# Sample attention: a stick chunk's weights are turned in the third tick behind its scores instead of the second

## The chip, the cores and the metric

The kernel runs on one core of a Trainium2 chip. The metric is device time in microseconds (us), median of several runs. The engines are named as in the profile: PE is TensorE (PEld its weight loads), DVE is VectorE, ACT is ScalarE, POOL is GpSimd, SP is SyncE, which only issues DMAs here. Each engine works through its own list of instructions in the order in which the program was written; between engines only semaphores hold.

## The reference, cut to what matters

Two decoder layers run over 512 prompt tokens and 64 sample tokens (8 requests of 8). Each layer is a SwiGLU FFN, a token mixing with four head groups (mLSTM, GLA, dilated window attention, stick-breaking attention), and a second FFN. The change touches only the sample's attention, whose stick-breaking part is this, for keys of 2048 past positions in pages and 8 new ones:

```python
z = q @ k.T * HEAD_DIM ** -0.5 + bias
log_beta = where(valid, log_sigmoid(z), -inf)
log_keep = where(valid, log_sigmoid(-z), 0)
later = cumsum(log_keep, reverse=True) - log_keep
out = exp(log_beta + later) @ v
```

## The kernel before

`program` loops twice (`nc.Fori`) over `ffn`, `mixing`, `ffn`. `mixing` projects, and then runs four stages one after the other, each closed by a barrier of all engines: `mlstm`, `rotary`, `gla` and `prompt_attention`. Those are the main work. Beside them the sample's attention is woven in as **side work**, cut into 62 ticks: `weave` writes, on each engine, some steps of the main stage, then the side ticks that `paced` assigns to that place, then main steps again. Ticks 0 to 25 lie in `mlstm`, 26 and 27 in `rotary`, 28 to 39 in `gla`, 40 to 61 in `prompt_attention` (`PACE`). So the order on an engine is fixed in the source, and a side instruction that waits holds up the main instruction behind it.

The side work takes four passes: stick-breaking for requests 0 to 3 and 4 to 7, then window attention for the same two groups. A **unit** is one tile of 128 past positions; tick t turns the keys of unit t. Four units of a stick pass form a **chunk** (m), scored into one PSUM bank; the new positions are a chunk of their own. In the order of a tick:

- PE: `turn_keys` (L2382, eight transposes, half into bank a, half into bank b), `score_unit` for the unit before (L2399), `turn_weights` of a chunk if its turn is due (L2429), `gather_rows` one tick behind the end of a pass (L2461), and `value_unit` (L2448, or L2442 for new positions).
- ACT: copy of bank a's keys (L2493), Exp of the chunk whose scores came the tick before (L2512), then Abs, Exp, Ln of a chunk just scored (L2518, L2520, L2522), the copy of the turned weights for an even m (L2501), the copy of the gathered rows (L2532).
- DVE: copy of bank b's keys (L2552), the running sum of the chunk before (L2598, L2601, L2604), the reading of a chunk's scores (L2579, L2570), the copy of the turned weights for an odd m (L2560), the output rows of a pass that ends (L2632).
- SP: the values of unit n + 4 are loaded when unit n has been multiplied (L2319, L2307). POOL gathers the keys of unit t + 4.

Bank a and bank b are one PSUM bank each. Keys and turned weights share them, so `turn_weights` waits until the keys of its own tick have been copied out of its bank, and the keys of the next tick wait until the weights have been copied out. `copy_weights_a` and `copy_weights_b` are these copies.

When a chunk is turned is decided in `side_plan`. A stick chunk m has its tick (1, 4, 8, 12, 16 in the first pass; 17, 20, 24, 28, 32 in the second), in which its scores are read. Its weights are `a_ready` when ACT has done L2512, one tick on. The plan is `turn_at` (before: ticks 3, 6, 10, 14, 18 and 19, 23, 26, 30, 34), and `value_at` has the products of a chunk in the four ticks behind its turn. The main lines that matter: L1497, L1518 (mLSTM, PE), L1462 (its Exp, ACT), L1399 (its product, DVE), L1210 and L1197 (the turning of a stage's result at its end, PE and ACT), L1129/L1131 (rotary, PE), L1821 (GLA, PE), L1735 and L1844 (GLA, DVE and PE), L1995, L2037 and L2057 (prompt attention).

Of the kernel before, what the change touches and what calls it, by code (L numbers as in the profile page):

```python
# [2152 lines left out]
def side_plan():  # L2153

    passes, units, chunks = [], [], []
    nth = {"stick": 0, "window": 0}
    for p, (kind, g) in enumerate(SIDE_ORDER):
        window = kind == "window"
        tiles = WIN_TILES if window else N_PAGES
        groups = [tuple(range(c, min(c + UT, tiles))) for c in range(0, tiles, UT)]  # L2160
        groups = groups + [()] if window else [()] + groups[::-1]
        first, unit0 = len(chunks), len(units)
        end = unit0 + tiles
        for k, group in enumerate(groups):
            m = len(chunks)
            tick = len(units) + len(group)
            if not group and not window:
                tick += 1
            chunks.append(dict(m=m, p=p, k=k, new=not group, window=window, g=g, tiles=group, unit0=len(units),
                               tick=tick, stick=None if window else nth["stick"], first=k == 0,  # L2170
                               last=k == len(groups) - 1, width=len(group) * P if group else NS))
            if not window:
                nth["stick"] += 1
            units += [(m, i, t) for i, t in enumerate(group)]
        passes.append(dict(kind=kind, window=window, g=g, unit0=unit0, end=end, chunk0=first, chunks=len(groups),
                           row=nth["window"] if window else None))
        if window:
            nth["window"] += 1


    turn_at, value_at, unit_at = {}, {}, [None] * len(units)
    done = []
    t_value = t_turn = 0
    for c in chunks:
        q = passes[c["p"]]
        ready = chunks[q["chunk0"] + q["chunks"] - 1]["tick"] + 2 if c["window"] else c["tick"] + 2
        t = max(ready, t_turn, done[c["m"] - 2] if c["m"] >= 2 else 0)
        turn_at.setdefault(t, []).append(c["m"])
        t_turn = t
        t_value = max(t_value, t + 1)  # L2190
        if c["new"]:
            value_at.setdefault(t_value, []).append((c["m"], None))
        for i in range(len(c["tiles"])):
            n = c["unit0"] + i
            value_at.setdefault(t_value, []).append((c["m"], n))
            unit_at[n] = t_value
            if t_value < len(units) or i % 2 == 1:
                t_value += 1
        done.append(t_value)
    ends = {}  # L2200
    for t in sorted(value_at):
        for m, n in value_at[t]:
            if chunks[m]["last"] and (n is None or n == chunks[m]["unit0"] + len(chunks[m]["tiles"]) - 1):
                ends[t] = chunks[m]["p"]
    ticks = max(ends) + 2


    events = {"a": {}, "b": {}}
    for t in range(ticks):
        if t < len(units):  # L2210
            for bank in "ab":
                events[bank]["k", t] = len(events[bank])
        for m in turn_at.get(t, ()):
            bank = "ab"[m % 2]
            events[bank]["p", m] = len(events[bank])
        if t - 1 in ends:
            events["a"]["g", ends[t - 1]] = len(events["a"])
    scored = {}
    for t in range(1, len(units) + 1):
        q = passes[chunks[units[t - 1][0]]["p"]]  # L2220
        if not q["window"] and t - 1 == q["unit0"]:
            scored["new", q["chunk0"]] = len(scored) + 1
        scored["unit", t - 1] = len(scored) + 1
        if q["window"] and t == q["end"]:
            scored["new", q["chunk0"] + q["chunks"] - 1] = len(scored) + 1
    valued = {}
    for t in sorted(value_at):
        for m, n in value_at[t]:
            valued["new", m] = valued["unit", n] = len({v for v in valued.values()}) + 1
    return dict(passes=passes, units=units, chunks=chunks, turn_at=turn_at, value_at=value_at, ends=ends, ticks=ticks,  # L2230
                events=events, scored=scored, valued=valued)


def sample_attention(nc, st, E, M, l, I, C):

    ps = E["ps"]
    DQT, DKT = M["TR"][:, DQ:DQ + 2, :], M["TR"][:, DK:DK + H, :]
    G = side_plan()
    passes, units, chunks = G["passes"], G["units"], G["chunks"]
    U, NP_ = len(units), len(G["passes"])  # L2240
# [723 lines left out]
```

## Time and profile before

| what | us |
|---|---|
| median of 3 runs | 2821.46 |
| lowest, highest | 2819.78, 2826.64 |
| the profiled execution's own time | 2828.29 |
| its span from first to last instruction | 2826.7 |
| PE busy | 2430.4 (86%) |
| DVE busy, ACT busy | 1249.8 (44%), 923.7 (33%) |

The profile is one execution. Its page gives sums for each engine and a row of digits in 40 slices of 70.7 us; the mixings with the side work lie in slices 9 to 14 and 28 to 34. All else comes from the timeline, which lists instructions by start, duration, engine and line, and says for some what the engine waited for. Start times in the text are those of the first layer.

### The profile page before, as it was taken

What the parts mean: (1) busy time and instruction counts of PE and PEld (TensorE: products, weight loads), DVE (VectorE), ACT (ScalarE), POOL (GpSimd) and SP (SyncE); (2) the same over time, 40 slices, a digit from 0 to 9 for tenths busy, and PEclk for the clock granted to TensorE, in tenths of its full rate; (3) what the DMA queues carried; (4) which work ended last, traced back from release to release, by engine and by line L of the source; (5) the groups of instructions that cost most, each with busy time, mean ns of one, the idle gap of its engine ahead of it and who ended that gap; (6) DMA issues with size and microseconds to landing.
All of it is one profiled execution on the core that took longest, in us unless ns stands there. A gap on an engine that the chain in (4) does not pass through costs nothing. (4 is left out here: it accounts for less than half of the span.)

```text
span 2826.7 us, 45166 instructions
## 1 busy us (share of the span) xinstructions
PE 2430.4 (86%) x17622; PEld 2140.8 (76%) x17622; DVE 1249.8 (44%) x2054; ACT 923.7 (33%) x1617; POOL 208.5 (7%) x279
## 2 busy tenths in 40 slices
PE   5999979969687877999879998898885786889996
PEld 5999968746445576999879998876563464889996
DVE  6433273143565536333354334521555555463324
ACT  4222232123424544222242223221343254432222
POOL 2000020011122001000010000100111110000000
PEclk7999989979787998999979999999896788899998
DMA  3223213155544442233223231322564444322332
GB/s 95 78 76 97 77 44 112 45 159 161 149 143 140 127 124 57 74 78 90 61 61 81 76 95 54 102 75 76 161 184 127 143 119 117 104 60 74 89 90 64
DMA packets 364348, 278.34 MB, mean 98 GB/s; under 512 B 51680, under 2 KB 347784, under 8 KB 363664
## 3 DMA queue, kind: packets, MB, share of 16 engines
q1 hardware_dynamic: 348048, 221.52, 27.8%
q0 software_dynamic: 16128, 54.54, 6.5%
q8 instruction: 106, 1.74, 0.3%
q14 instruction: 66, 0.54, 0.1%
HBM read 262.41 MB, written 13.58 MB: 98 GB/s over the span
## 5 line engine op out<-in xcount | busy, mean ns | idle before, releaser
L216 PE MATMUL ps<-h_hi,w_hi 128*128 128x288 f32 x2400 | 739.5, 308 | 133.6 <-PEq L172 47.2
L217 PE MATMUL ps<-h_lo,w_hi 128*128 128x288 f32 x2400 | 724.6, 302 | 0.0
L218 PE MATMUL ps<-h_hi,w_lo 128*128 128x288 f32 x2400 | 723.8, 302 | 0.0
L216 PEld LDWEIGHTS ps<-h_hi,w_hi 128*128 128x128 f32 x2400 | 465.6, 194 | 152.7 <-issue 71.7
L217 PEld LDWEIGHTS ps<-h_lo,w_hi 128*128 128x128 f32 x2400 | 466.9, 195 | 1.2
L218 PEld LDWEIGHTS ps<-h_hi,w_lo 128*128 128x128 f32 x2400 | 466.2, 194 | 0.0
L240 DVE TENSOR_TENSOR w_lo<-w_raw,w_hi 128x2048 fp32r<-128x2048 f32 x133 | 306.5, 2305 | 299.1 <-ACT w_hi L234 299.0
L234 ACT ACTIVATE w_hi<-w_raw 128x2048 fp32r<-128x2048 f32 x133 | 253.4, 1905 | 167.8 <-PE ps L218 161.3
L216 PE MATMUL ps<-f_a_hi,w_hi 128*128 128x288 f32 x1024 | 302.7, 296 | 0.0
L218 PE MATMUL ps<-f_a_hi,w_lo 128*128 128x288 f32 x1024 | 301.6, 295 | 0.0
L217 PE MATMUL ps<-f_a_lo,w_hi 128*128 128x288 f32 x1024 | 301.5, 294 | 0.0
L696 ACT ACTIVATE f_gate<-f_gate 128x288 f32<-128x288 f32 x128 | 56.9, 444 | 473.7 <-DVE f_gate L726 473.6
L216 PEld LDWEIGHTS ps<-f_a_hi,w_hi 128*128 128x128 f32 x1024 | 192.0, 188 | 0.4
L217 PEld LDWEIGHTS ps<-f_a_lo,w_hi 128*128 128x128 f32 x1024 | 192.0, 188 | 0.2
L218 PEld LDWEIGHTS ps<-f_a_hi,w_lo 128*128 128x128 f32 x1024 | 192.0, 188 | 0.0
L2382 PE MATMUL ps<-ident,sa_kn 128*128 128x128 f32 x832 | 140.3, 322 | 38.2 <-DMA sa_kn<-in_cache_sb_k,page_rows 14.9
L726 DVE TENSOR_TENSOR f_gate<-ps,f_inv_x 128x288 f32<-128x288 f32 x128 | 58.5, 457 | 233.5 <-PE ps L218 233.3
L2382 PEld LDWEIGHTS ps<-ident,sa_kn 128*128 128x128 f32 x832 | 115.2, 169 | 60.9 <-issue 36.8
L394 POOL TENSOR_TENSOR A<-A,f_x_sq 128x288 f32<-128x288 f32 x56 | 44.7, 798 | 1323.2 <-ACT f_x_sq L384 1323.2
L216 PE MATMUL ps<-w_hi,h_hi 128*128 128x512 f32 (+1 forms) x320 | 126.7, 396 | 0.0
L2552 DVE COPY sa_kt<-ps 128x512 f32<-128x512 f32 x104 | 71.7, 690 | 124.1 <-PE ps L2382 121.6
L217 PE MATMUL ps<-w_lo,h_hi 128*128 128x512 f32 (+1 forms) x320 | 124.9, 390 | 0.0
(348 smaller groups left out, 3357.9 us busy)
## 6 DMA issues: line engine op xcount, KB each, us to landing
w_raw<-in_w_ffn_in SPq DMA_DIRECT2D x132, 512.0 KB, 5.2
w_raw<-in_w_ffn_out SPq DMA_DIRECT2D x64, 512.0 KB, 4.9
sa_vn<-in_cache_sb_v SPq DMA_DIRECT2D x256, 128.0 KB
w_raw<-in_w_in SPq DMA_DIRECT2D x52, 512.0 KB, 4.6
sa_kn<-in_cache_win_k POOLq DMA_DIRECT2D x96, 128.0 KB, 3.3
sa_vn<-in_cache_win_v SPq DMA_DIRECT2D x96, 128.0 KB
sa_kn<-in_cache_win_k POOLq DMA_DIRECT2D x16, 512.0 KB, 4.8
sa_vn<-in_cache_win_v SPq DMA_DIRECT2D x16, 512.0 KB
```

Source lines behind the costliest of these rows:

```text
L216: pe.matmul(out, stat_hi, mov_hi, start=start, stop=False, skip_group_check=True)
L217: pe.matmul(out, stat_hi, mov_lo, start=False, stop=False, skip_group_check=True)
L218: return pe.matmul(out, stat_lo, mov_hi, start=False, stop=stop, skip_group_check=True)
L234: act.activation(E["w_hi"][:, slot], E["w_raw"][:, slot], ACT.Copy).then_inc(S["w_hi"], 1)
L240: dve.tensor_tensor(E["w_lo"][:, slot], E["w_raw"][:, slot], E["w_hi"][:, slot].bitcast(F32), ALU.subtract).then_inc(S["w_lo"], 1)
L394: pool.tensor_tensor(E["acc_x"][:, hs], E["acc_x"][:, hs], F["xsq"][:, N.adds(n) % 2], ALU.add).then_inc(S["x_added"], 1)
L696: act.activation(gate[:, j, :], gate[:, j, :], ACT.Silu).then_inc(S["silu_done"], 1)
L726: dve.tensor_tensor(gate[:, j, :], E["ps"][:, PAIR[j], 0:HALF], inv_x[:, half_of(j // 2)], ALU.mult).then_inc(S["scaled"], 1)
L2382: mm = pe.transpose(ps[:, banks[e % len(banks)], j * P:(j + 1) * P], kn[:, n % SLOTS, j, pair * P:(pair + 1) * P], E["ident"][:])
L2552: dve.tensor_copy(kt[:, n % 2, 1], ps[:, TURN_B[e % len(TURN_B)], :]).then_inc(S["free_b"], 1)
```

## The change

One number of the plan: a stick chunk is ready to be turned three ticks after its scores, not two. The new positions' chunks are stick chunks too. Window chunks keep their rule.

```diff
@@ side_plan
     for c in chunks:
         q = passes[c["p"]]
-        ready = chunks[q["chunk0"] + q["chunks"] - 1]["tick"] + 2 if c["window"] else c["tick"] + 2
+        ready = chunks[q["chunk0"] + q["chunks"] - 1]["tick"] + 2 if c["window"] else c["tick"] + 3
         t = max(ready, t_turn, done[c["m"] - 2] if c["m"] >= 2 else 0)
         turn_at.setdefault(t, []).append(c["m"])
```

The ten stick turns then stand in ticks 4, 7, 11, 15, 19, 20, 24, 27, 31 and 35, all stick products one tick later than before, the ends of the two stick passes in ticks 23 and 40 instead of 22 and 39, and their gathers in 24 and 41 instead of 23 and 40. From tick 44 on everything stands where it stood, and there are 62 ticks as before. Nothing is added or removed. Keys, scores, Exp, Ln and sums keep their ticks; POOL's list is the same.

**PE at the end of `mlstm`, ticks 23 to 25, before** (L1578 and L1210 are main, the rest side):

```order
L2382 MATMUL ps<-ident,sa_kn 128x128 x8
L2399 MATMUL ps<-sa_kt,sa_qb 32x128 x8
L2429 MATMUL ps<-ident,sa_zs 128x128 x4
L2461 MATMUL ps<-sa_gather,sa_rows 128x32 x2
L2442 MATMUL ps<-RB,sa_pT 128x256
L1578 MATMUL ps<-ident,A 4x64
L1579 MATMUL ps<-ident,sa_zw 16x128
L2382 MATMUL ps<-ident,sa_kn 128x128 x8
L2399 MATMUL ps<-sa_kt,sa_qb 32x128 x8
L2448 MATMUL ps<-sa_vn,sa_pT 32x256 x4
L1210 MATMUL ps<-ident,ml_room 128x128 x8
```

The same stretch of the change:

```order
L2382 MATMUL ps<-ident,sa_kn 128x128 x8
L2399 MATMUL ps<-sa_kt,sa_qb 32x128 x8
L2448 MATMUL ps<-sa_vn,sa_pT 32x256 x4
L1578 MATMUL ps<-ident,A 4x64
L1579 MATMUL ps<-ident,sa_zw 16x128
L2382 MATMUL ps<-ident,sa_kn 128x128 x8
L2399 MATMUL ps<-sa_kt,sa_qb 32x128 x8
L2429 MATMUL ps<-ident,sa_zs 128x128 x4
L2461 MATMUL ps<-sa_gather,sa_rows 128x32 x2
L2442 MATMUL ps<-RB,sa_pT 128x256
L1210 MATMUL ps<-ident,ml_room 128x128 x8
```

The turn of chunk 6, the gather of the first pass and the product of chunk 5 moved from the tick ahead of L1578 to the tick ahead of L1210.

**ACT at the same place**, as a piece of the difference:

```order
 L2522 ACT_TABLE_LOAD
 L2522 ACTIVATE sa_f<-sa_f 128x512
+L2501 ACTIVATE sa_pT<-ps 128x512
+L2532 ACTIVATE TR<-ps 128x2x32
 L1197 ACTIVATE TR<-ps 128x128 x8
 L1197 ACTIVATE TR<-ps 128x64 x2
```

The two copies that belong to them now stand behind the Ln of chunk 7 (L2522) and ahead of the main copies L1197.

**PE at the start of `gla`'s main products, ticks 30 and 31** (L1821 is main):

```order
 L2382 MATMUL ps<-ident,sa_kn 128x128 x8
 L2399 MATMUL ps<-sa_kt,sa_qb 32x128 x8
+L2448 MATMUL ps<-sa_vn,sa_pT 32x256 x4
+L2382 MATMUL ps<-ident,sa_kn 128x128 x8
+L2399 MATMUL ps<-sa_kt,sa_qb 32x128 x8
 L2429 MATMUL ps<-ident,sa_zs 128x128 x4
-L2448 MATMUL ps<-sa_vn,sa_pT 32x256 x4
-L2382 MATMUL ps<-ident,sa_kn 128x128 x8
-L2399 MATMUL ps<-sa_kt,sa_qb 32x128 x8
 L2448 MATMUL ps<-sa_vn,sa_pT 32x256 x4
 L1821 MATMUL ps<-ident,A 128x128
```

The turn of chunk 8 moved behind the keys and scores of the next tick; both ticks stand ahead of L1821 either way.

## Rows read from the trace of the kernel before

**Rows 1.** The page: PE's granted clock in 40 slices, in tenths of 2.4 GHz.

```profile
PEclk7999989979787998999979999999896788899998
```

**Rows 2.** Windows, ticks 0 to 51 of each layer: length, busy by engine, clock, DMA.

```profile
584.08:945.40 361.32, 278.31 (x2371) 189.02 (x2370) 193.84 (x419) 138.57 (x298) 58.64 (x84) 0.82 0.52 153
1969.93:2336.63 366.70, 278.69 (x2371) 187.64 (x2370) 194.05 (x419) 138.48 (x298) 58.51 (x84) 0.82 0.52 151
```

**Rows 3.** Line L2429: what ended PE's idle time before it (us, times).

```profile
  issue: 45.9, 24
  ACT sa_kt L2493: 21.3, 6
  DVE sa_kt L2552: 14.4, 6
```

**Rows 4.** Timeline, ticks 3 and 4: start, duration, engine, line [idle <-releaser].

```profile
607.29 0.39 PE L2429 MATMUL ps<-ident,sa_zs 128*64 128x128 f32 x1 [4.77 <-ACT sa_kt L2493]
...
608.13 1.94 PE L2382 MATMUL ps<-ident,sa_kn 128*128 128x128 f32 x8 [0.45 <-ACT sa_pT L2501]
...
611.13 1.22 PE L2442 MATMUL ps<-RB,sa_pT 64*128 64x256 f32 x2
...
612.28 0.87 PEld L1497 LDWEIGHTS ps<-ident,ml_room 4*128 4x128 f32 x8 [0.65 <-issue]
```

**Rows 5.** Timeline, ticks 6 and 7.

```profile
625.68 0.63 PE L2429 MATMUL ps<-ident,sa_zs 128*128 128x128 f32 x4 [1.91 <-DVE sa_kt L2552]
...
626.35 0.69 DVE L2560 COPY sa_pT<-ps 128x512 f32<-128x512 f32 x1 [0.81 <-PE ps L2429]
...
630.11 0.61 PE L1518 MATMUL ps<-ml_mask,ident 128*128 128x128 f32 x2
...
631.07 0.68 DVE L2552 COPY sa_kt<-ps 128x512 f32<-128x512 f32 x1
```

**Rows 6.** Timeline, tick 24 and the end of `mlstm`.

```profile
738.62 0.69 PE L1210 MATMUL ps<-ident,ml_room 128*128 128x128 f32 x2 [6.36 <-DVE ml_room L1181]
739.11 0.63 ACT L2522 ACTIVATE sa_f<-sa_f 128x512 f32<-128x512 f32 x1
739.65 0.42 ACT L1197 ACTIVATE TR<-ps 128x128 f32<-128x128 f32 x2
739.96 0.69 PE L1210 MATMUL ps<-ident,ml_room 128*128 128x128 f32 x2 [0.65 <-ACT TR L1197]
740.47 0.49 ACT L1197 ACTIVATE TR<-ps 128x128 f32<-128x128 f32 x2 [0.40 <-PE ps L1210]
```

**Rows 7.** Timeline, tick 26, in `rotary`.

```profile
757.75 1.02 DVE L1095 TENSOR_TENSOR x<-ro_tmp 128x256 f32<-128x256 f32 x4
...
759.53 0.63 PE L2429 MATMUL ps<-ident,sa_zs 128*128 128x128 f32 x4 [4.03 <-DVE sa_kt L2552]
...
761.10 0.48 PE L1129 MATMUL ps<-ident,x 128*128 128x128 f32 x1
```

**Rows 8.** Timeline, ticks 30 and 31, in `gla`.

```profile
789.30 0.64 ACT L2512 ACTIVATE sa_zs<-sa_zs 128x512 f32<-128x512 f32 x1 [3.35 <-DVE sa_zs L2604]
...
794.83 1.09 PE L2429 MATMUL ps<-ident,sa_zs 128*128 128x128 f32 x4 [5.08 <-ACT sa_kt L2493]
...
796.87 1.97 PE L2382 MATMUL ps<-ident,sa_kn 128*128 128x128 f32 x8
...
800.74 0.46 PE L1821 MATMUL ps<-ident,A 128*128 128x128 f32 x1
```

**Rows 9.** Timeline, ticks 34 and 35, in `gla`.

```profile
828.75 1.45 PE L1837 MATMUL ps<-x,gl_room 64*128 64x256 f32 x4 [0.41 <-DVE gl_room L1735]
...
834.08 0.27 DVE L1735 COPY gl_room<-ps 64x128 f32<-64x128 f32 x1
```

**Rows 10.** Timeline, end of pass 1 in tick 39, and its gather in tick 40.

```profile
863.84 0.41 DVE L2632 TENSOR_TENSOR sa_rows<-ps,sa_head_cols 128x256 f32<-128x256 f32 x1
...
878.16 1.06 PE L2461 MATMUL ps<-sa_gather,sa_rows 128*128 128x32 f32 x4
```

## The prediction

> **What bounds the kernel now.** I read the page's clock row first, then windows over the two mixings, then the answer for line L2429, then the timeline around each of the ten stick turns, in both layers. The clock row shows where engines wait for each other: it is 9 in the FFNs and falls to 7 and 8 in the mixings, since PE's clock falls to 1.2 GHz where PE has idled [rows 1]. Over ticks 0 to 51 PE is busy for 278 of 361 us, DVE for 194, ACT for 139 [rows 2]. No engine is full there: PE's own list sets the pace in the middle of `mlstm`, and a chain through DVE and ACT does so at the start and the end of each stage. What a moved turn is worth therefore depends on which engine is late at its old and its new place.
>
> The change gives the weights' Exp a tick more. I looked whether that is what the turn waits for. It is not. For chunk 8, Exp ends at 789.94 and the turn starts at 794.83 [rows 8]; in all 20 stick turns of both layers, Exp ends 2.7 to 10.5 us ahead. What the turn waits for, where it waits, is the copy that empties its bank of the keys of its own tick: ACT's L2493 or DVE's L2552 [rows 3]. Both come late only where those engines have main work ahead of them. In the first layer this is 4.77 us in tick 3 [rows 4], 1.91 in tick 6 [rows 5], 4.03 in tick 26 [rows 7] and 5.08 in tick 30 [rows 8]; at the other six turns PE stands still for at most 0.4 us. A turn in the next tick waits for the copy of that tick's keys by the same rule. So the change replaces waits, it doesn't remove a dependency.
>
> **The change, place by place.** Times are of the first layer; each sum is a shift of the main work behind it, plus is later.
>
> Ticks 3 to 7, the start of `mlstm`. With no turn in tick 3 the keys of tick 4 still wait for the same bank; they start where the turn started, 607.29, not at 608.13: -0.85 [rows 4]. From tick 4 the product of chunk 0 goes (L2442 to the next start, 1.15) and the turn comes in (about 0.35), so L1497 starts 1.65 sooner; the product stands in tick 5 now and takes 1.15 back. That leaves -0.5. In tick 6 DVE is the late engine: it loses the copy L2560 and the wait ahead of it (0.69 + 0.81 = 1.5), so its key copy of tick 7, which ends at 631.75, ends at 629.75 [rows 5]. There the turn now waits for it: 629.75 + 0.15 + 0.65 = 630.55 for L1518, which starts at 630.11 now. **+0.4.** The 0.15 is the step from a copy to PE, 0.65 the turn's own length [rows 5].
>
> Ticks 10 to 20, PE sets the pace. Each of the turns of chunks 2 to 5 leaves a tick where it costs PE its own 0.65 and enters one where it costs the same; the copies find ACT and DVE with room in both. Zero. If that room were gone at one of them, it is one copy, 0.6 to 0.7, as in tick 6 [rows 5].
>
> Tick 24, the end of `mlstm`. This is the largest term. Turn 6, the gather and the product of chunk 5 were in tick 23, where PE had time to spare while DVE normalised. Now they stand between the scores of tick 24 and L1210. Turn 6 itself fits: L1210 waits for DVE until 738.62 in any case. But its copy L2501 is written behind the Abs, Exp and Ln of chunk 7 on ACT, with two table loads among them, and Ln ends at 739.74 [rows 6]. The gather needs the same bank and must wait for L2501. Before, ACT went from Ln straight to L1197. Now follow: L2501 about 0.6, the step to PE 0.15, the gather 1.06 at the low clock [rows 10], the product of chunk 5 1.15 [rows 4], and 0.5 from the start of L1210 to ACT's L1197 (739.96 to 740.47 [rows 6]). The sum, 0.6 + 0.15 + 1.0 + 1.15 + 0.5, is **+3.4**: L1197 starts at 743.1 instead of 739.65. Everything to the stage's end hangs on it: keys 25, their product, SP's last value load, the barrier. At its cheapest (the gather and product at 2.4 GHz, half as long) it is 2.3; nothing hides it, since the two L1210 that were done early are now behind it.
>
> Ticks 26 and 27, `rotary`. L1129 needs only DVE's L1095, which ends at 758.77, but stands behind the turn, which waits until 759.53, and the product, and starts at 761.10 [rows 7]. Without the turn the product is done in the idle time, and L1129 starts at 758.95: -2.15. In tick 27 the turn finds its bank copied and costs its 0.65. **-1.5.**
>
> Ticks 30 and 31, `gla`. PE stands for 5.08 us until ACT has copied key tile 30, then works off turn, product, keys 31 (1.97), scores, product, and reaches L1821 at 800.74 [rows 8]. The change does the product in the idle time, but keys 31 wait for the same copy. They start at 794.85 instead of 796.87, and the turn (1.09) and one product (1.0) follow them: 794.85 + 1.95 + 1.1 + 1.1 + 1.0 = 800.0 for L1821. Of 5.08 us of idle time the change wins **-0.7**.
>
> Ticks 34 and 35, `gla`. Tick 34 loses the wait, the turn and with them 1.35 us ahead of L1837 (828.75, could start at 827.4 [rows 9]). Tick 35 gets them: 0.15 + 0.65 on PE, then DVE copies the weights (0.69) ahead of L1735, so that this starts at 835.6 instead of 834.08 [rows 9]; +1.55. **+0.2.**
>
> Ticks 40 and 41, `prompt_attention`. The pass's last product takes the gather's place on PE, about as long as its 1.06 [rows 10], but DVE's L2632 (0.41) must wait for it ahead of the main L2037: 0.4 of wait and 0.4 of work. The gather comes into tick 41 ahead of L1995, 1.06, of which DVE is late by more than half anyway: 0.45. **+1.25.** The nearest bounds are 0 (this stage hides both) and 1.9.
>
> The sum is 0.4 + 3.4 - 1.5 - 0.7 + 0.2 + 1.25 = +3.05 per layer, **+6.1 us** for both layers, since all waits stand in the second layer too. On the profiled execution (2828.29) that gives 2834.4, and on the median of the runs, 6.8 below it, 2821.46 + 6.1 = **2827.5 us**.
>
> What this can't contain is where PE's clock falls. The same 2371 matmuls of ticks 0 to 51 took 361.32 us in one layer and 366.70 in the other, at the same mean clock [rows 2]. So the places at which the low clock lands are worth about 5 us per mixing, in either direction, and any shift of a few us moves them.
>
> **The rivals.** A measurement of this kernel tells about 0.3% from no change, 8.5 us, so the bounds are 2813.0 and 2829.9.
>
> *Slower: the losses count and the gains don't.* The mechanism is the one of tick 24: a copy of turned weights that stands behind chunk 7's table functions on ACT and holds L1210. It decides if the -2.15 of tick 26 and the -0.7 of tick 31 are absorbed, for instance if `rotary` ends on SP's value load rather than on PE. Then a layer pays 0.4 + 3.4 + 0.65 + 0.2 + 1.25 = 5.9, both 11.8: 2833. From 4.2 per layer on it is a loss that can be measured; the sum stands at 3.05, so 1.2 us more per layer is enough, and the clock's share alone is larger. For it speaks that all its terms are lists in strict order; against it that PE and DVE, not SP, work last in `rotary`.
>
> *Faster: the idle time was the bound.* The four waits and the two small ones of a layer sum to 16.2 us; at the new places I find 2.4 (tick 7) and 3.6 (tick 24), 6.3 in all. If the main work followed PE's idle time one for one, 9.9 per layer would be won: 2801.7. Against it: keys 4 and keys 31 wait for the same copies that the turns waited for [rows 4, 8]. A part of it, 4.2 per layer, would be enough to be seen.
>
> The row that bears on the clock is this: at 794.83 a turn takes 1.09 after 5.08 idle, the same turn in tick 6, after 1.91 idle, takes 0.63 [rows 5, 8]. The Trainium skill (TensorE: Matmul & The Clock Gate, "What's actually happening") says that the throttled state is the default and that activity releases it; by that rule a plan with less idle time on PE in ticks 3, 26 and 30 would win beyond the waits. As a mechanism here: if the keys of ticks 4, 25 to 28 and 31 ran at the high clock (1.09 for 1.97, 0.9 each) and the products with them, some 5 to 8 us per layer; with the sum above that is 2818 to 2812. Against it stands tick 24, where PE idles longer than before, until 740.5.
>
> *The change does nothing of note* is inside the forecast: a layer's sum near zero gives 2821.5.
>
> **How the numbers follow.** The forecast, within 0.3%, has 0.53: its sum of +6 leaves 2.4 us to the upper bound and 14.5 to the lower, with 5 to 7 us of scatter by the clock. Slower has 0.35, nearly all of it from the tick 24 mechanism with the clock against it. Faster has 0.12: 0.04 for the idle time as the bound, 0.08 for the clock's gain. The range, 8 in 10, reaches from the sum less 12.5 (the gains in full, tick 24 at 2.3, the last stage hiding its part, a layer's clock in favour) to the sum plus 11.5 (the slower rival with a layer's clock against): 2815 to 2839.
>
> **What would show it.** In tick 24, L2501 should start as Ln ends, L2461 0.75 later, and L1210 some 4 us later against the stage's start than before; if L2501 comes before Ln, the largest term is wrong. L1129 in tick 26 should follow L1095 at once. PE's idle time ahead of L2429 should fall from 21.3 and 14.4 us to a few, with L2382 named in its stead for ticks 4 and 31. If L1497 to L1518 shift by more than 1 us, the first term is wrong. The prediction as a whole fails if the two mixings change by over 4 us each.

## The result, and the profile after

The changed kernel takes 2836.64 us (median of 13 runs, 2828.33 to 2850.22). The kernel before takes 2824.84 us beside it (13 runs, 2816.38 to 2828.03). The ratio is 1.0046, with a 95% interval of 1.0033 to 1.0060: slower by about 12 us, a loss that can be told from no change. A second timing, in another batch, gave 1.0038 (1.0022 to 1.0054). The forecast was 2827.5 us. The time lies in its range, but it is the rival "slower" that came about, not the likeliest case.

The profiled execution of after took 2829.22 us (span 2827.6), 7 us under its median; the one of before took 2828.29. So this pair of traces shows the places, but not the full size of the loss. The change was traced a second time, in an execution of 2838.02 us, close to its median; where that trace says something else, it is named. First the page's clock row of after, then its windows over ticks 0 to 51 in each layer (columns as in [rows 2]: length, PE, PEld, DVE, ACT and POOL busy, granted clock, DMA share, GB/s).

```profile
PEclk7999989969786988999979999999797897899998
```

```profile
582.15:952.45 370.30, 284.44 (x2371) 193.94 (x2370) 194.27 (x419) 138.30 (x298) 58.78 (x84) 0.80 0.51 149
1974.14:2336.19 362.05, 271.08 (x2371) 185.06 (x2370) 193.93 (x419) 138.16 (x299) 58.81 (x84) 0.84 0.53 153
```

The same 2371 matmuls: 370.30 us against 361.32 in the first layer, 362.05 against 366.70 in the second [rows 2]. One layer lost 9.0 us and the other won 4.65. PE's busy time goes the same way (284.44 and 271.08, before 278.31 and 278.69), and so does the clock, 0.80 and 0.84 of full speed. Two layers of one execution differ by 8.25 us, about as much as the change moved either of them. In the second trace the same two stretches took 367.15 and 367.85 us: 5.8 and 1.2 us more than before, 7.0 in all.

Next, what ended PE's idle time before the turns (L2429), and before the key transposes (L2382), in after:

```profile
  ACT sa_kt L2493: 9.9, 6
  DVE sa_kt L2552: 6.2, 4
```

```profile
  ACT sa_kt L2493: 26.4, 10
  DVE sa_kt L2552: 12.7, 11
```

and the second of these in before:

```profile
  DVE sa_kt L2552: 8.6, 8
  ACT sa_kt L2493: 6.1, 6
```

Before the turns the wait for the two copies fell from 35.7 us [rows 3] to 16.1, of which 8.8 stand at chunk 6's new place in tick 24, 4.40 in each layer. Before the keys it rose from 14.7 to 39.1. In all 50.4 us became 55.2: the wait wasn't removed, it went over to the next instruction that needs the bank. (Idle time without a releaser went the same way, 45.9 to 26.0 us before the turns and 36.8 to 55.4 before the keys.)

**The start.** Keys 4, the first main line, and the main line of tick 7 (start, duration, engine, line, idle time and releaser):

```profile
605.52 1.94 PE L2382 MATMUL ps<-ident,sa_kn 128*128 128x128 f32 x8 [4.74 <-ACT sa_kt L2493]
...
608.88 1.12 PE L1497 MATMUL ps<-ident,ml_room 4*128 4x4 f32 x10
```

```profile
628.63 0.64 PE L1518 MATMUL ps<-ml_mask,ident 128*128 128x128 f32 x2
629.06 1.91 PE L1520 MATMUL ps<-ml_arow,ml_sel 128*128 128x512 f32 x2
```

The first layer's list starts 1.93 us sooner than in before (keys 0 at 581.00 and 582.93). On before's scale L1497 stands at 610.81 (worked out: 610.63) and L1518 at 630.56 (worked out: 630.55). In this layer these steps held to 0.2 us. In the second layer L1497 comes 1.8 us sooner than in before, and L1518 1.8 us later, where the sum had 0.4; before's own two layers have L1518 at 47.18 and 46.09 us from their keys 0. So that the first layer fits to 0.01 us is luck in part. Over all traces the term holds in the mean: 46.65 us in the fourteen layers with the first pass late, 46.19 in the twelve with before's first pass, +0.46 (the kernels are those of the experiments below; the one that alters tick 7 isn't counted).

What the sum didn't have is the line behind it. L1520 takes 1.91 us in tick 7 here; this is the same line in before:

```profile
630.55 1.02 PE L1520 MATMUL ps<-ml_arow,ml_sel 128*128 128x512 f32 x2
```

The clock was still low when the main work came. In thirteen of those fourteen layers this L1520 took 1.88 to 1.92 us, in one 1.02 (second trace, second layer); in the twelve others 1.02 to 1.40.

**Tick 24.** ACT's table functions, the copy behind them, the gather, the product of chunk 5, L1210 and L1197:

```profile
742.53 0.63 ACT L2522 ACTIVATE sa_f<-sa_f 128x512 f32<-128x512 f32 x1
743.07 0.58 ACT L2501 ACTIVATE sa_pT<-ps 128x512 f32<-128x512 f32 x1
...
743.79 1.03 PE L2461 MATMUL ps<-sa_gather,sa_rows 128*128 128x32 f32 x4 [4.20 <-ACT sa_pT L2501]
744.75 1.22 PE L2442 MATMUL ps<-RB,sa_pT 64*128 64x256 f32 x2
...
745.90 0.69 PE L1210 MATMUL ps<-ident,ml_room 128*128 128x128 f32 x2
746.41 0.49 ACT L1197 ACTIVATE TR<-ps 128x128 f32<-128x128 f32 x2 [1.33 <-PE ps L1210]
```

From the end of Ln (743.16) to L1197 are 3.25 us; the sum had 3.4.

**Rotary and `gla`.** L1129 now follows L1095 (which ends at 765.43) at once; from the start of `rotary` it stands at 6.6 us, 2.3 sooner than in before, where the sum had 2.15. In tick 31, keys, turn, product and L1821:

```profile
765.48 0.33 PE L1129 MATMUL ps<-ident,x 128*128 128x128 f32 x1 [2.48 <-DVE x L1095]
```

```profile
799.86 1.94 PE L2382 MATMUL ps<-ident,sa_kn 128*128 128x128 f32 x8 [5.87 <-ACT sa_kt L2493]
...
802.86 1.11 PE L2429 MATMUL ps<-ident,sa_zs 128*128 128x128 f32 x4
803.91 1.08 PE L2448 MATMUL ps<-sa_vn,sa_pT 128*32 128x256 f32 x8
804.92 0.34 PE L1821 MATMUL ps<-ident,A 128*128 128x128 f32 x1
```

As foreseen the keys have taken over the turn's wait (5.87, before 5.08 ahead of the turn [rows 8]). Against the stage's start L1821 comes 0.5 us sooner.

**What the lists don't say.** The same stage a little later, tick 33: first the first layer of after, then the second.

```profile
822.07 2.49 PE L1837 MATMUL ps<-x,gl_room 64*128 64x256 f32 x4 [2.68 <-DVE gl_room L1735]
...
824.49 1.97 PE L1844 MATMUL ps<-x,gl_room 128*128 128x64 f32 x8
```

```profile
2212.30 1.45 PE L1837 MATMUL ps<-x,gl_room 64*128 64x256 f32 x4 [2.67 <-DVE gl_room L1735]
2213.68 1.10 PE L1844 MATMUL ps<-x,gl_room 128*128 128x64 f32 x8
```

Same instructions, same idle time ahead, one execution; 4.46 us in one layer, 2.55 in the other. The one ran at the low level of the clock (1.2 GHz), the other at the high one (2.4 GHz). What did differ is the stretch ahead: in the first layer turn 8 and its product took 1.11 and 1.08 us, and L1821 started 28.4 us after the stage's start, in the second 27.3. This goes together in all fourteen traces of this document: where L1821 stood at 27.1 to 27.5 us, this L1837 took 1.45 (fourteen layers); where it stood at 27.9 to 29.2, it took 2.4 to 2.5 (thirteen layers, and one exception with 1.45). It is a regularity; no run here changed one of the two alone. `gla` as a whole took 96.34 and 92.47 us, in before 96.98 and 98.00.

**Ticks 41 and 42, `prompt_attention`.** After, and then the two lines of before that answer to its second and fourth:

```profile
891.91 1.06 PE L2461 MATMUL ps<-sa_gather,sa_rows 128*128 128x32 f32 x4
892.79 0.77 PE L1995 MATMUL ps<-TR 128*128 128x128 f32 x2
893.36 0.95 PE L2014 MATMUL ps<-RB,pa_pT 128*128 128x64 f32 x4
...
897.72 1.92 PE L2382 MATMUL ps<-ident,sa_kn 128*128 128x128 f32 x8
```

```profile
887.07 0.49 PE L1995 MATMUL ps<-TR 128*128 128x128 f32 x2
...
890.77 1.05 PE L2382 MATMUL ps<-ident,sa_kn 128*128 128x128 f32 x8
```

From this L1995 to keys 42 there are 4.93 us in after and 3.70 in before. The gather itself (1.06, ahead of this L1995) is one loss; that the lines behind it run at the low clock (L1995 0.77 for 0.49, and so on to keys 1.92 for 1.05) is a second, of the same size. In the second layer of this trace the lines behind the gather ran at the high clock, and from keys 41 to keys 42 only 0.4 us were lost, against 2.6 in the first; both layers of the second trace lost 2.4 to 2.6.

### The profile page after: what moved, and what is told of

Its sections match the earlier page's. It is cut to its first block and busy times, and to the rows that moved or that the text cites. A ratio compares the mean times of both kernels' runs of the same rounds, so it can differ in the third digit from the quotient of the medians.

```text
span 2827.6 us, 45166 instructions
## 1 busy us (share of the span) xinstructions
PE 2426.6 (86%) x17622; PEld 2140.7 (76%) x17622; DVE 1250.3 (44%) x2054; ACT 923.5 (33%) x1617; POOL 209.2 (7%) x279
## 3 DMA queue, kind: packets, MB, share of 16 engines
q1 hardware_dynamic: 348048, 221.52, 27.9%
## 5 line engine op out<-in xcount | busy, mean ns | idle before, releaser
L2382 PE MATMUL ps<-ident,sa_kn 128*128 128x128 f32 x832 | 141.4, 324 | 61.4 <-ACT sa_kt L2493 26.4
L2382 PEld LDWEIGHTS ps<-ident,sa_kn 128*128 128x128 f32 x832 | 116.6, 170 | 83.5 <-issue 55.4
```

Of the source, the lines that this page charges most:

```text
L2382: mm = pe.transpose(ps[:, banks[e % len(banks)], j * P:(j + 1) * P], kn[:, n % SLOTS, j, pair * P:(pair + 1) * P], E["ident"][:])
```

## The experiments

Each kernel ran in five rounds beside the kernel before, on the same chip as it; there were four batches, on three chips. A difference between kernels of two batches is therefore taken from their two ratios. The edits are in `side_plan`, where not said otherwise. "Gives 5 us" is the ratio times 2825.

**Parts of the change.** The start alone: the first pass's chunks 0 to 5 are turned a tick later, and the last two products of chunk 4 share tick 22, so that nothing moves from tick 23 on.

```diff
-        ready = ... c["tick"] + 2
+        ready = ... c["tick"] + (3 if c["m"] < 6 else 2)
-            if t_value < len(units) or i % 2 == 1:
+            if n != 14 and (t_value < len(units) or i % 2 == 1):
```

> Only the first pass's chunks 0 to 5 are turned a tick later (ticks 4, 7, 11, 15, 19, 20); two products share tick 22, so that the pass still ends in tick 22, turn 6 and the gather stay in tick 23, and everything behind stands as in the kernel before. It is the first term alone. Theory of the lists (a turn costs what waits in its list): L1518 in tick 7 comes 0.4 us later and the rest of mlstm keeps that, at most 1.1 with the second product in tick 22: +1 to +2 us in all, a ratio of 1.0005. Theory of the clock (the idle time moved to tick 7 puts mLSTM's first products at 1.2 GHz): from tick 7 to tick 12 another 3 to 4 us per layer, as in the profile of the change (keys of tick 12 are 4.3 and 4.2 us late there), +8 to +9 us in all, a ratio of 1.003.

Measured: 1.0018 (1.0007 to 1.0029), +5 us, between 2 and 8. Where the sum had +0.8 for both layers, and the shared tick 22 could add little, the start costs several times that. Its one trace, of its fastest execution (2823.65 us), doesn't show the loss: its two mixings are as long as before's.

The second pass alone, `(3 if c["m"] >= 6 else 2)`. Chunk 6 stays in tick 23, since its turn waits for the products of chunk 4 in any case; so chunks 7, 8 and 9 move, and no product does.

> Only the second pass's chunks 6 to 9 are ready a tick later. Chunk 6 stays in tick 23, since it waited for chunk 4's products already; chunks 7, 8 and 9 are turned in ticks 27, 31 and 35; no product moves. These are the terms of rotary and gla alone: -1.5 (ticks 26, 27), -0.7 (30, 31), +0.2 (34, 35), so -2.0 per layer, -4 us in all, a ratio of 0.9986. In the profile of the change rotary was 1.98 and 1.91 us shorter and gla 0.64 and 5.5; if that holds, -5 to -8 us. If the gain was only the barrier's (rotary short since mlstm ended late), rotary stays at 19.6 us and the ratio at 1.

Measured: 0.9964 (0.9952 to 0.9977), -10 us. This part of the change is a gain, two and a half times the sum's -4.0. Tick 31 in its first layer:

```profile
793.28 1.94 PE L2382 MATMUL ps<-ident,sa_kn 128*128 128x128 f32 x8 [4.53 <-ACT sa_kt L2493]
...
796.29 0.67 PE L2429 MATMUL ps<-ident,sa_zs 128*128 128x128 f32 x4
796.88 0.64 PE L2448 MATMUL ps<-sa_vn,sa_pT 128*32 128x256 f32 x8
797.45 0.33 PE L1821 MATMUL ps<-ident,A 128*128 128x128 f32 x1
```

The list is after's; turn and product take 0.67 and 0.64 for 1.11 and 1.08. The clock rose before them here, and behind them there. `gla` took 93.51 and 92.64 us.

The change with ACT's copy of the turned weights written ahead of Abs, Exp and Ln:

```diff
+        for m in G["turn_at"].get(t, ()):
+            if m % 2 == 0:
+                copy_weights_a(act, chunks[m])
         ... Abs, Exp, Ln of weighed_at(t, 0) ...
-        for m in G["turn_at"].get(t, ()):
-            if m % 2 == 0:
-                copy_weights_a(act, chunks[m])
```

> The change, with ACT's copy of turned weights (L2501) written ahead of Abs, Exp and Ln of its tick instead of behind them. In tick 24 the copy then follows the turn at about 736.4, the gather is released 4 us sooner, and L1210 may start by 738.7; what is left is that Ln, and so L1197, comes 1.1 us later. Theory of the lists: the 3.4 us of tick 24 fall to 1.1 per layer, 4.6 us less than the change in all, a ratio of about 1.003 to the kernel before; mlstm ends 2.3 us sooner than in the change. Rival (L1210 is held by the gather and the product of chunk 5 themselves, not by the place of the copy): mlstm's end as late as in the change.

Measured: 0.9999 (0.9985 to 1.0013). Writing the copy first gives back 11 to 13 us of the change's loss, where the list had 4.6. The queue behind Ln is a real cost, but not all of this: from keys 23 to keys 25 the trace has 20.96 us, the change 22.74 and before 19.38. That is 1.8 us a layer won in tick 24 (the list: 2.3), 3.6 in all. The rest lies in other stretches and isn't explained by the list.

The change with the keys of unit 7 transposed twice over (no work left out):

```diff
-            for j in range(SG):
+            for j in tuple(range(SG)) * (2 if n in (7,) else 1):
```

> The change, with the eight key transposes of tick 7 done twice (same data, same bank), so that PE works in the 2.4 us in which it waits for DVE there. Nothing else is added, and the second set ends before DVE's key copy can (DVE is late at that place), so the lists cost nothing, or 0.5 us at most. Theory of the clock: PE keeps or regains 2.4 GHz at L1518, the keys of tick 12 are 2 to 4 us less late than in the change, and the time falls by up to 8 us, to a ratio of 1.001 to 1.003. Theory of the lists, or of a clock that doesn't depend on this idle stretch: keys of tick 12 stay 4 us late and the ratio at 1.0046.

Measured: 1.0034 (1.0021 to 1.0047) beside 1.0046 for the change. The intervals overlap; the time tells nothing apart. The trace shows more. In its first layer the added transposes didn't shorten the wait before the turn of tick 7 (2.44 us; in the change's four traced layers 2.42 to 3.02), and L1520 took 1.91. In its second layer the wait fell to 1.52 us, L1520 took 1.02, and the keys of tick 22 came 0.7 us later than in before instead of 2.9 to 5.4. That is what the clock theory said, but it is one layer, and the change's second trace has a layer with L1520 at 1.02 behind a wait of 2.55.

The change itself again, and the first pass alone with all its products late, `(3 if c["m"] < 6 else 2)`:

> The changed kernel itself again, unaltered, beside the three below: a second trace of it, and its time against the runs of before of this batch. By adding the parts that have been timed apart (mlstm's start alone +5, the second pass alone -10, and by the lists twice +3.4 in tick 24 and twice +1.25 in ticks 40 and 41) it would stand only 4 us over before, ratio 1.0015. Theory 'parts add up, and the first timing of the change was an unlucky draw of the clock': 2829, 1.0015, and in the trace mlstm some 3 us shorter than the 177.88 and 176.60 us of its first trace. Theory 'the change has a loss of its own that the parts don't show': 2836 to 2838 again, 1.0045, and the keys of tick 22 again 4 to 5 us later than before's in both layers, where the two kernels that make the start alone or copy first show 0 to 3.

> Only the six chunks of the first pass are turned a tick later; since chunks 4 and 5 end later, chunk 6 goes to tick 24, and all stick products move as in the change. Chunks 7, 8 and 9 stay in ticks 26, 30 and 34. So the losses of the sum stand (A, B, F) and its gains (C in rotary, D in gla) are left out. If the parts add up: +5 for the start, twice 3.4 for tick 24, twice 1.25 for ticks 40 and 41: 14 us over before, ratio 1.005, and 10 us over the change by what the second pass alone gave. If the change's second pass gives nothing when its first pass is there too, the ratio is the change's, 1.0045. In the trace gla should be before's 97 to 98 us, against 92.5, and rotary 20 against 18.

Measured: 1.0038 (1.0022 to 1.0054), so the first timing was no accident; and 1.0091 (1.0075 to 1.0107), +26 us, where the sum had 2 x (0.4 + 3.4 + 1.25) = +10. Windows of the first-pass kernel over `prompt_attention` in both layers, then of the change with its last two products in one tick (the next kernel):

```profile
876.64:1025.76 149.12, 110.44 (x894) 78.51 (x894) 72.43 (x165) 74.24 (x177) 11.34 (x20) 0.79 0.42 123
2275.47:2425.01 149.54, 110.99 (x894) 78.69 (x894) 72.41 (x165) 74.25 (x177) 11.34 (x20) 0.79 0.42 123
```

```profile
871.65:1012.52 140.87, 102.99 (x887) 73.40 (x887) 71.66 (x164) 74.45 (x177) 11.39 (x20) 0.84 0.44 126
2264.25:2405.55 141.30, 103.07 (x887) 73.33 (x887) 71.68 (x164) 74.47 (x177) 11.39 (x20) 0.84 0.43 126
```

The first two windows hold one product more and 8 us more time: the clock stood at 0.79 against 0.84 of full speed. From tick 40 on the lists of the first-pass kernel are those of the change, and yet the change took 142.4 to 145.0 us there, 4 to 7 less. So the cost of F depends on what ran ahead of it.

**The gather of tick 41.** The change, but the last two stick products share tick 39, `if n != 30 and (...)`, so that the gather stands in tick 40 as before.

> The change, but the last two stick products share tick 39, so that the stick pass is gathered in tick 40 as before and not in 41. By my sum this takes term F away: -1.25 a layer, 2833.5 where the change itself measured 2836, ratio 1.003. Theory 'prompt attention's stretch follows the clock': in the kernels timed so far it ran for 140 to 149.5 us a layer with the same instructions but for this move, and the six layers with the late gather and tick 42's keys at 24.6 us or later from its first load all show a low clock from 14 to 28 us there. If the move brings that spell about, the stretch falls from 144 to 141 to 142 us with it: 5 us in all, 2831, ratio 1.002.

Measured: 1.0020 (1.0005 to 1.0035), 5 to 7 us less than the change (1.0038 and 1.0046); the three intervals overlap, so this difference is at the edge of what can be told. `prompt_attention` took 140.87 and 141.30 us, in the change's two traces 144.06, 142.41, 144.17 and 144.96.

**Single chunks of the second pass.** Chunks 7 and 8 late, `(3 if c["m"] in (7, 8) else 2)`, and chunk 8 alone, `(3 if c["m"] == 8 else 2)`:

> Of the second pass only chunks 7 and 8 are turned a tick later (ticks 27 and 31); chunk 9 stays in tick 34. My term E held moving chunk 9 for a loss of 0.2 us a layer. Theory 'gla's 4.5 us belong to chunk 8 (list and, behind it, the clock)': as the second pass whole or a little better, 2817, ratio 0.9963, gla 92 to 93.5 us. Theory 'part of it belongs to chunk 9, whose product stood in the way of the scan of ticks 33 to 35': gla about 95 us, and 2821, ratio 0.998.

> Only chunk 8 is turned a tick later (tick 31 instead of 30), one move of the twenty that the change makes. By my sum it is term D alone, -0.7 a layer, 2823, ratio 0.9995. If the 4.5 us that gla gained in three other kernels come from it: -9, 2816, ratio 0.997, gla 92 to 93.5 us, and rotary's stretch as before, 19.6 to 20.2. If the clock's gain in ticks 33 and 34 hangs on a shift that begins in tick 26 (chunk 7), gla gains only the 1.6 to 1.8 us a layer of the list: 2821.5, ratio 0.9988.

Measured: 0.9956 (0.9942 to 0.9969) and 0.9975 (0.9966 to 0.9984). Chunk 8 alone gives 7 us where the sum had 1.4, and chunk 7 some 5 on top (the sum: 3), though the two intervals overlap. Chunk 9 gives nothing that can be told (0.9956 without it, 0.9964 with it); the sum had +0.4 for it. `gla` took 94.82 and 95.01 us with chunk 8 alone: 2.6 us a layer less than before.

**An experiment that didn't do what it was for.** The kernel before with the keys of unit 33 transposed twice over, `(2 if n == 33 else 1)`:

> The kernel before, with the eight transposes of unit 33's keys done twice over in tick 33 of each sample attention: 1.07 us more of TensorE's work per layer, laid into an idle time of 2.68 us before L1837 (which waits for VectorE's L1735). No list moves. Theory 'lists': hidden, ratio 1.000 (2825 to 2826). Theory 'clock': in before L1837, L1844 and L1825 after that idle time ran at half clock (2.49, 1.97 and 1.91 us against 1.45, 1.10 and 1.02 in the group ahead), in the kernels with chunk 8 late only the first of them did. If a shorter idle time lifts the clock there, more work makes the kernel faster: -1.8 to -4 us a layer, 2818 to 2821, ratio 0.998, gla 93 to 95 us instead of 97 to 98.

Measured: 0.9998 (0.9984 to 1.0011). Its L1837 in the first and in the second layer:

```profile
819.30 2.39 PE L1837 MATMUL ps<-x,gl_room 64*128 64x256 f32 x4 [2.68 <-DVE gl_room L1735]
```

```profile
2209.45 1.45 PE L1837 MATMUL ps<-x,gl_room 64*128 64x256 f32 x4 [2.68 <-DVE gl_room L1735]
```

The idle time is 2.68 us as before, not 1.6. DVE's copy of the keys stands ahead of L1735 on DVE, so the extra 0.88 us of transposes moved L1735 too and lay on the path. It doesn't decide whether less idle time lifts the clock. It shows again that after one and the same idle time the clock is low once and high once; its second layer is the exception named above, high although L1821 came late. The 1.8 us for both layers are less than the interval (4 us either way) can show.

**Can it be better?** The fastest so far with ACT's copy written first:

> The fastest kernel so far (chunks 7 and 8 late, 0.9956) with ScalarE's copy of the turned weights written ahead of the Abs, Exp and Ln of its tick, as in the copy-first kernel. In the first pass chunks 4 and 6 and in the second chunk 8 are copied by ScalarE, chunk 6 in tick 23, where Abs, Exp and Ln stand ahead of it and cost table loads. Lists: 0 to -2 a layer, ratio 0.994 to 0.9956 (2808 to 2813). Clock: any shift may tip a spell either way, 0.993 to 0.998.

Measured: 0.9965 (0.9950 to 0.9980); no better. Last, the change with units 14 and 15 sharing tick 22 (`if n != 14 and (...)`), which leaves all turns late but chunk 6's, and puts products, chunk 6 and gather back:

> The change with the last two products of chunk 4 sharing tick 22. All ten chunks are turned a tick later except chunk 6, which keeps tick 23, and the products, chunk 6 and the gather of tick 40 are before's: terms B (tick 24) and F (ticks 40 and 41) leave together, A, C, D and E stay. By adding what was timed apart (start alone 1.0018, second pass alone 0.9964): 0.998, 2820 to 2823 beside a before of 2825 to 2829. Theory 'one layer's clock is handed on to the next stage, so that parts don't add': anything from 0.996 to 1.003. By the trace: tick 24 to 25 as before (13.5 us from keys to keys), rotary 17.5 to 19.5, gla 92 to 96, prompt attention 141 to 142.5, and mlstm 170 to 173 us.

Measured: 0.9984 (0.9971 to 0.9998). The parts timed apart, 1.0018 and 0.9964, had said 0.9982. Its windows over `mlstm`, `rotary`, `gla` and `prompt_attention` of the first layer:

```profile
583.38:756.21 172.83, 133.36 (x1197) 92.55 (x1197) 81.85 (x162) 64.40 (x122) 25.41 (x26) 0.84 0.57 169
756.21:775.87 19.66, 12.67 (x88) 8.09 (x88) 11.66 (x47) 3.81 (x12) 1.87 (x2) 0.71 0.38 110
775.87:869.65 93.78, 68.38 (x525) 40.99 (x525) 58.78 (x106) 27.01 (x51) 19.81 (x36) 0.82 0.55 151
869.65:1010.40 140.75, 103.08 (x886) 73.34 (x886) 71.63 (x164) 74.27 (x177) 11.34 (x20) 0.84 0.44 127
```

So nearly the whole loss hangs on what this edit takes back: chunk 6 in tick 24, the pass's end in ticks 40 and 41, and the second pass's products, which stand a tick late in between. The last alone don't cost it: the copy-first kernel keeps them late and has `gla` at 92.5 and 93.8 us. Without these collateral moves the same idea is slightly faster than before.

The mean of the two layers' stage lengths in each trace, in us (from such windows and the first instructions of the stages):

| kernel | `mlstm` | `rotary` | `gla` | `prompt_attention` | ratio |
|---|---|---|---|---|---|
| before | 169.1 | 19.9 | 97.5 | 143.2 | 1 |
| change, first trace | 177.2 | 18.0 | 94.4 | 143.2 | 1.0046 |
| change, second trace | 175.6 | 17.5 | 96.0 | 144.6 | 1.0038 |
| start alone | 169.5 | 19.7 | 97.7 | 142.8 | 1.0018 |
| first pass | 176.2 | 20.0 | 97.6 | 149.3 | 1.0091 |
| second pass | 169.5 | 19.0 | 93.1 | 141.8 | 0.9964 |
| chunks 7, 8 | 169.8 | 18.0 | 94.9 | 143.0 | 0.9956 |
| chunk 8 | 169.8 | 18.8 | 94.9 | 145.3 | 0.9975 |
| copy first | 173.2 | 18.3 | 93.1 | 145.7 | 0.9999 |
| last two products | 176.1 | 17.7 | 96.0 | 141.1 | 1.0020 |
| unit 7 twice | 173.8 | 19.6 | 92.6 | 142.4 | 1.0034 |
| unit 33 twice | 169.7 | 20.1 | 96.4 | 142.1 | 0.9998 |
| chunks 7, 8, copy first | 169.5 | 18.4 | 93.8 | 141.1 | 0.9965 |
| tick 22 shared | 173.2 | 19.5 | 93.7 | 140.8 | 0.9984 |

A row is one execution, and some aren't typical: the traced one of unit 7 twice was the fastest of its six, 12 us under their median.

**A version that beats both** is the one with chunks 7 and 8 alone turned late: 2813.51 us (2809.56 to 2818.23) beside 2825.44, 0.9956. It ran only five times, and the whole second pass late isn't told apart from it.

## Why the prediction was right in its signs and wrong in its size

Take the terms for both layers together, as the sum had them and as the runs price them:

| term | sum | timed | from |
|---|---|---|---|
| A, start of `mlstm` | +0.8 | +5 | start alone |
| B, tick 24 | +6.8 | about +10 | change less tick 22 shared (15 to 18), less F |
| C + D + E, ticks 26 to 35 | -4.0 | -10 | second pass alone |
| F, ticks 40 and 41 | +2.5 | +5 to +7 | change less last two products |
| sum | +6.1 | +11 to +13 | the change itself |

B is what is left of the whole when the others are taken off, so that the parts meet the sum proves nothing; and each timed part is uncertain by 3 to 6 us, B by more. With that said, the signs of A, of C + D + E and of B + F are right, and the sizes are too small, by 1.5 to 6 times in the middle of the intervals.

**What held.** The model of the lists. L1497 and L1518 stood within 0.2 us of where they were worked out to be in the first layer, and L1518 in the mean of all. Tick 24 is right in mechanism and size: between the keys of ticks 23 and 25 all ten layers of five traces with this plan (the change twice, the first pass, the last two products, unit 7 twice) lost 3.3 to 3.4 us against before, and the kernel with tick 22 shared lost none. L1129 follows L1095 at once, and `rotary` took 18.4 us in the mean of the eighteen layers with chunk 7 late, 19.7 in the ten others; but in the kernels with unit 7 twice and with tick 22 shared it took 19.4 to 19.7 all the same. Keys 31 took over the turn's wait, and after's own first layer wins 0.5 us at L1821. The copy-first kernel confirms the queue behind Ln, for 1.8 of its 3.4 us.

**What failed: the term of the clock.** The text put the clock outside the sum, as scatter of 5 to 7 us "in either direction". It isn't only scatter; part of it goes with the plan and comes again in trace after trace:

- A. The keys of tick 22 come 2.3 to 5.4 us later than in before in twelve of the fourteen layers that carry the first pass late, and -0.2 and +1.6 in the two of the start-alone kernel, 3.2 in the mean; in ten layers of five kernels with before's first pass they differ by -0.3 to +1.5, 0.5 in the mean. (The kernel with unit 7 twice isn't counted; it has 2.7 and 0.7.) So the start costs some 2.7 us a layer, not 0.4. It arises behind L1518: this line is 0.46 us later in the mean, the keys of tick 12 are 3.0 later, those of tick 22 2.8. The lists have nothing there; what differs is the clock, at L1520 in tick 7 as shown above and again at keys 10, which took 1.26 to 1.91 us in twelve of the fourteen layers and 1.04 or 1.05 in eleven of the twelve others. So the step that failed is "Ticks 10 to 20 ... Zero" with the end of the one before it: +0.4 a layer was worked out, about 2.7 was measured. The rows of keys 10 in the change's second trace and in before:

```profile
646.01 1.91 PE L2382 MATMUL ps<-ident,sa_kn 128*128 128x128 f32 x8
```

```profile
645.77 1.04 PE L2382 MATMUL ps<-ident,sa_kn 128*128 128x128 f32 x8
```

- D. The list gave 0.7 us at L1821, and 0.5 in the change's first layer. The six layers of the second-pass, chunks-7-8 and chunk-8 kernels had L1821 1.0 to 1.8 us sooner against the stage's start, by turn and product at the high clock. From the L1837 of tick 33 to the keys of tick 34 there are 6.9 to 7.1 us where L1837 ran at the low clock, and 5.2 to 5.6 where it ran at the high one. How much of it a layer gets differs: the change's own four layers took 96.3, 92.5, 95.9 and 96.2 us.
- F. From keys 41 to the next L1995 it is 3.73 us in after and 2.37 in before (keys at 889.06 and 884.70). 0.44 of it is L2399 at the low clock, the other 0.9 the gather, of which DVE's lateness was to leave 0.45; and the lines behind it ran at the low clock, as shown above. Timed, it is about 3 us a layer, where 1.25 was worked out, and above the upper bound of 1.9. Against before's own `prompt_attention`, which took 141.04 us in one layer and 145.40 in the other, the traces alone would not show it; the timed kernel points to it, at the edge of its interval.
- B's extra is not in tick 24. Of the eight layers with the late tick 24 and the second pass late (the change twice, the last two products, unit 7 twice) five have `gla` at 96 and three at 92.5; the four with tick 24 mended (copy first, tick 22 shared) have 92.5 to 93.8. That a stage hands on a state of the clock to the next would fit this, but it is argued, not shown; where B's extra comes from stays open.

**The rivals.** "Slower" came about, but not by its mechanism: it had the losses as computed and the gains absorbed, +11.8 us in all. That +11.8 is also the difference of the two medians is luck: the gains weren't absorbed (second pass alone, -10 us), and the losses were larger than computed. Its threshold was right: "1.2 us more per layer is enough, and the clock's share alone is larger". It should have had more weight for that. "Faster: the idle time was the bound" can't be the whole, since PE's waits for the two copies rose from 50.4 to 55.2 us; in the second pass alone they fell to 40.9, by 9.5, and the time fell by 10. For that part no run sets less idle time apart from what the lists and the clock gave.

The clock's rival had named places. The keys of ticks 25, 27 and 31 were to run at the high clock; in after's first layer they took 1.97, 1.94 and 1.94 us, the low one. The Trainium skill (TensorE: Matmul & The Clock Gate, "What's actually happening") calls the throttled state the default, which activity releases. The first half of that is what the rows behind the longest waits show here (keys 31 behind 5.87 us: 1.94). But the two L1837 after 2.67 and 2.68 us of idle time, one at either level, show that the wait directly ahead doesn't settle it, and by this rule alone the change's sign could not be had.

**By its own tests.** "The prediction as a whole fails if the two mixings change by over 4 us each": they changed by +9.0 and -4.65 in the first trace and by +5.8 and +1.2 in the second, so it fails. The sums of the two, +4.3 and +7.0, are near the +6.1 that was worked out, and say nothing for it. L1518 shifted by 1.8 us in the second layer, over the 1 us that was to show the first term wrong. The signs set for tick 24 came as written: L2501 starts as Ln ends, L2461 0.72 us later, and L1210 3.9 us later against keys 23. Against the stage's start it is 9.2 us later, since the keys ahead were late already.

## What to carry to other kernels

Where engines wait for each other in short pieces, work out the lists to find signs and culprits, but don't take their sum for the size: here the timed parts came out at 1.5 to 6 times their list terms, and where the traces show the difference it is PE's clock. A rule applied to all chunks alike can be a gain at some of them (here 7 and 8) and a loss at the others; look for what it drags along (a product schedule that shifts, a pass whose end slips into the next stage), and time the parts apart before dropping the idea. A wait for a shared bank goes to the next user of the bank when the first is moved away.

## What the runs showed of the hardware

- PE's clock falls in much the same places in traces of one plan, but two layers of one execution with the same instructions may differ: `gla` by 3.9 us (96.34 and 92.47), `prompt_attention` of before by 4.4 (141.04 and 145.40).
- The effects of parts on the time added up within their intervals: start alone and second pass alone gave 0.9982 together, measured 0.9984; first pass and second pass gave 1.0055, measured 1.0046 and 1.0038.
- A chain of eight transposes takes 1.04 to 1.10 us at the high level of the clock and 1.91 to 1.97 at the low one; a gather, 1.01 to 1.07 us at the low one and 0.58 to 0.60 at the high one.
- The same four products L1837, behind the same 2.67 or 2.68 us of idle time, ran at either level (1.45 us in fifteen traced layers, 2.39 to 2.50 in thirteen); the level went with how early L1821 had come in the stage.
